# Reordering the down projection of a two-layer trunk: operand sums behind the seventh pair, an own buffer for a weight chunk, one low part on VectorE, and the first row's weighting

## The reference

```
h = RMSNorm(x);  z = h @ W_in
A = gMLP spatial gating;  B = differential attention
x = x + RMSNorm(concat(A, B) @ W_out)
h = RMSNorm(x);  gu = h @ W_gate_up         # 1024 -> 2 x 2816
y = (silu(gate) * up) @ W_down              # 2816 -> 1024
x = x + RMSNorm(y) * post_ffn_g
```

## Time and profile before

| | |
|---|---|
| median of 3 runs | 1087.85 us (1087.07 to 1088.01) |
| the profiled execution | 1088.94 us |
| its span, first to last instruction | 1087.1 us |
| mean granted TensorE clock, as a share of full speed | 0.995 |
| busy share: PE, DVE, ACT, POOL | 98%, 72%, 58%, 46% |
| down projection and its residual, layer 0 | about 423 to 545 us of the span |
| the same, layer 1 | 960 us to the end |

### The profile page before, as it was taken

The page is one execution under the profiler, slowest core; times in us unless marked ns, Lnnn a source line. Parts: engine busy times, 40 slices in busy tenths (PEclk is TensorE's granted clock), DMA queues, the critical chain, the costliest instruction groups (busy, mean ns, idle before and its releaser), DMA issues.

```text
span 1087.1 us, 17807 instructions
## 1 busy us (share of the span) xinstructions
PE 1064.4 (98%) x6704; PEld 950.4 (87%) x6704; DVE 781.7 (72%) x1267; ACT 632.3 (58%) x1253; POOL 501.8 (46%) x386
## 2 busy tenths in 40 slices
PE   9999999999999999999899999999999999999997
PEld 7888788999999999778678888889999999987775
DVE  4376554878888885978754756457888888869784
ACT  6767784755555554434457568656555555544361
POOL 3534364466666663020544344634766666610221
PEclk9999999999999999999999999999999999999999
DMA  9423113424433432664453222232343344336442
GB/s 297 139 61 108 65 59 88 145 79 117 117 109 88 115 118 78 225 210 160 141 159 104 78 78 78 78 129 85 99 118 107 90 115 116 95 121 233 154 165 77
DMA packets 151161, 130.39 MB, mean 120 GB/s; under 512 B 4250, under 2 KB 120484, under 8 KB 151076
## 3 DMA queue, kind: packets, MB, share of 16 engines
q1 hardware_dynamic: 151060, 129.25, 38.0%
q10 hardware_dynamic: 16, 0.00, 0.0%
HBM read 122.95 MB, written 6.29 MB: 119 GB/s over the span
## 4 chain that ended last, share of the span: by engine, by line
PE 81%; DVE 10%; DMA 3%; ACT 2%; POOL 2%; issue 2%; POOLq 0%; DVEq 0%; SPq 0%; ACTq 0%
PE banks L694 25%; PE banks L696 24%; PE banks L695 24%; DVE w_lo L2140 3%; DMA raw<-in_w_down_dram 2%; POOL w_lo L632 2%; PE banks L759 2%; PE banks L787 2%; PE banks L703 1%; PE banks L772 1%; PE banks L1012 1%; DVE raw L2127 1%; DVE raw L2129 1%; DVE part_full L2104 1%; DVE raw L2125 1%
## 5 line engine op out<-in xcount | busy, mean ns | idle before, releaser
L632 POOL TENSOR_TENSOR w_lo<-raw,w_hi 128x512 fp32r<-128x512 f32 x148 | 197.3, 1358 | 382.0 <-ACT w_hi L1222 382.0
L650 POOL TENSOR_TENSOR w_lo<-raw,w_hi 128x512 fp32r<-128x512 f32 x200 | 261.4, 1318 | 145.9 <-ACT w_hi L1303 141.5
L694 PE MATMUL banks<-xg_hi,w_hi 128*128 128x256 f32 (+1 forms) x880 | 273.5, 311 | 0.0
L696 PE MATMUL banks<-xg_lo,w_hi 128*128 128x256 f32 (+1 forms) x880 | 271.3, 308 | 0.0
L695 PE MATMUL banks<-xg_hi,w_lo 128*128 128x256 f32 (+1 forms) x880 | 271.2, 308 | 0.0
L1303 ACT ACTIVATE w_hi<-raw 128x512 fp32r<-128x512 f32 x200 | 124.6, 631 | 116.6 <-DVE raw L2034 64.2
L696 PEld LDWEIGHTS banks<-xg_lo,w_hi 128*128 128x128 f32 x880 | 168.1, 191 | 8.5
L694 PEld LDWEIGHTS banks<-xg_hi,w_hi 128*128 128x128 f32 x880 | 168.1, 191 | 8.2
L695 PEld LDWEIGHTS banks<-xg_hi,w_lo 128*128 128x128 f32 x880 | 168.1, 191 | 7.5
L696 PE MATMUL banks<-s_part,w_hi 128*128 128x256 f32 x480 | 135.8, 283 | 0.0
L694 PE MATMUL banks<-s_part,w_hi 128*128 128x256 f32 x480 | 135.8, 283 | 0.0
(11 more groups left out here) (225 smaller groups left out, 2175.0 us busy)
## 6 DMA issues: line engine op xcount, KB each, us to landing
raw<-in_w_gate_up_dram SPq DMA_DIRECT2D x88, 512.0 KB, 4.1
raw<-in_w_down_dram SPq DMA_DIRECT2D x58, 512.0 KB, 3.9
raw<-in_w_in_dram SPq DMA_DIRECT2D x40, 512.0 KB, 3.8
raw<-in_w_out_dram SPq DMA_DIRECT2D x16, 512.0 KB, 3.4
x_spill<-x_rows SPq DMA_DIRECT2D x8, 512.0 KB, 5.0
x_rows<-x_spill SPq DMA_DIRECT2D x8, 512.0 KB, 6.3
raw<-in_w_down_dram SPq DMA_DIRECT2D x14, 256.0 KB, 2.6
x_rows<-in_x_dram SPq DMA_DIRECT2D x4, 512.0 KB, 7.1
```

The lines of the kernel that those rows point to most:

```text
L632: last = tt(lo[:, piece], raw_half(l, c, h)[:, piece], hi[:, piece].bitcast(F32), ALU.subtract)
L650: tt(lo, full, hi.bitcast(F32), ALU.subtract).then_inc(w_ready, 1)
L694: mm(o, stat[0], mov[0], start=first, stop=False)
L696: return mm(o, stat[0], mov[1], start=False, stop=last)
```

## The change

- **Order on DVE.** `h_low(0)` moves behind the sums of P0. `h_low(1)`, `s4_sums(EARLY)` and `h_low(2)` move behind P6. `h_low(3)` moves behind the sums of Q0. On ACT `h_high(3)` moves behind L18's high parts and `keep_p1`.
- **R14's raw home.** Its halves no longer pass through `raw`: they have places of their own in `part_full`, are loaded right behind Q2 once P6's T3 product is done, and signal `r14_landed`. R18, now of kind Z, so follows Q6 in `raw` and reuses Q5's buffer. S1's high part moves one tile up and two buffers of `keep_p5` move, to make room.
- **Low part of R18's second half.** It is made on DVE (`late_low`, two pieces, semaphore `late_ready`), between `add_right(0)` and `add_p56(1)`. POOL then has six pieces for R14 and R18.
- **First row.** `gain_a` of row 2 runs behind the first row's add and that of row 3 behind its weighting, followed by `bias_a` for rows 2 and 3. `bias_a` for rows 0 and 1 comes with `gain_a` of those rows.

```diff
-        [("R", 14), ("R", 18)]
+        [("R", 14), ("Z", 18)]
...
+    C_R14 = C_DOWN + DOWN.index(("R", 14))
...
-                   "S1": (part_hi[:, NP:2 * NP, :], hid_hi[:, first_of_pair, right]),
+                   "S1": (part_hi[:, NP + 1:2 * NP + 1, :], hid_hi[:, first_of_pair, right]),
...
-        p5 = part_full[:, 0, 2 * NP:2 * NP + 2, :], part_full[:, 1, 2 * NP:2 * NP + 2, :]
+        p5 = part_full[:, 1, 2 * NP:2 * NP + 2, :], m1_full.rearrange("p (a q) -> p a q", a=2)
...
-        LOWS_OF = {"B": 5, "P": 0, "Q": 0, "W": 2, "L": 2, "R": 2}
+        LOWS_OF = {"B": 5, "P": 0, "Q": 0, "W": 2, "L": 2, "R": 2, "Z": 1}
...
+        RAW_ORDER = [(l, c) for l in range(L) for c in range(NC) if c != C_R14]
+
+        def raw_n(l, c):
+
+            return (NC - 1) * l + c - (c > C_R14)
+
         def raw_half(l, c, h):
-            return raw[:, (NC * l + c) % 2, h, :]
+            if c == C_R14:
+                return part_full[:, 0, 4 * h:4 * h + 4, :].rearrange("p n q -> p (n q)")
+            return raw[:, raw_n(l, c) % 2, h, :]
...
             def load_half(l, c, h):
-                n = NC * l + c
+                n = raw_n(l, c)
                 if n >= 2:
 
-                    m, d = divmod(n - 2, NC)
+                    m, d = RAW_ORDER[n - 2]
...
+                    elif d == LAST and h == 1:
+                        sp.wait_ge(late_ready, m + 1)
...
+            def load_r14(l):
+
+                sp.wait_ge(w_done, upto(l, C_P[NP - 1], P_T3))
+                for h in range(2):
+                    view, src = weights_of(l, C_R14, h)
+                    sp.dma_start(view(raw_half(l, C_R14, h)), src).then_inc(r14_landed[h], 16)
...
                 for c in range(C_DOWN + 2, NC):
+                    if c == C_R14:
+                        continue
                     load(l, c)
+                    if c == C_Q[2]:
+                        load_r14(l)
...
                     if not paired(c):
                         low(l, c, 0)
-                        low(l, c, 1)
+                        if c != LAST:
+                            low(l, c, 1)
...
-                pe.wait_ge(w_ready, low_upto(l, c, h))
+                if c == LAST and h == 1:
+                    pe.wait_ge(late_ready, l + 1)
+                else:
+                    pe.wait_ge(w_ready, low_upto(l, c, h))
...
-                    elif c == C_P[6]:
-                        h_high(3)
                     elif c == C_L_END:
                         keep_p1(0)
                         keep_p1(1)
+                        h_high(3)
...
-                if rows[-1] == ST - 1:
-                    ts(bias_a[:, :], ssq_a[:, :], 1.0 / D, EPS, ALU.mult, ALU.add).then_inc(bias_a_ready, 1)
+                if len(rows) > 1:
+                    add_eps(slice(rows[0], rows[-1] + 1))
+
+            def add_eps(at):
+
+                ts(bias_a[:, at], ssq_a[:, at], 1.0 / D, EPS, ALU.mult, ALU.add).then_inc(bias_a_ready, 1)
...
                     tt(y_b, y_b, silu_t[:, r, :], ALU.add).then_inc(y_b_added, 1)
+                    if r == 0:
+                        gain_a(b, (2,))
                 dve.wait_ge(ssq_b_ready, ST * b + r + 1)
                 tt(y_b, y_b, gpost[:, HALF:D], ALU.mult).then_inc(y_b_gained, 1)
+                if b % 2 and r == 0:
+                    gain_a(b, (3,))
+                    add_eps(slice(2, ST))
...
+                def late_low():
+
+                    hi, lo = high_low(l, LAST, 1)
+                    dve.wait_ge(w_hi_ready, upto(l, LAST, 1))
+                    for piece in (slice(0, CE // 2), slice(CE // 2, CE)):
+                        last = tt(lo[:, piece], raw_half(l, LAST, 1)[:, piece], hi[:, piece].bitcast(F32), ALU.subtract)
+                    last.then_inc(late_ready, 1)
...
-                h_low(0)
                 for p in range(NP):
                     pair_sums(C_P[p])
+                    if p == 0:
+                        h_low(0)
                     pair_lows(C_P[p])
                     if p < 2:
                         s2_sum(p)
-                    elif p == 4:
-                        h_low(1)
-                    elif p == 5:
-                        s4_sums(EARLY)
-                        h_low(2)
-                h_low(3)
+                s4_sums(EARLY)
+                h_low(1)
+                h_low(2)
                 add_p7(0)
                 add_p7(1)
                 pair_sums(C_Q[0])
+                h_low(3)
                 pair_lows(C_Q[0])
...
-                for j in range(2):
-                    add_p56(j)
-                    add_right(j)
+                add_p56(0)
+                add_right(0)
+                late_low()
+                add_p56(1)
+                add_right(1)
...
-                    gain_a(2 * l + 1, range(2, ST))
```

More of the change, by code:

```diff
@@ L128, in trunk @@
         silu_t = sb("silu_t", [P, 4, S])
-        m1 = sb("m1", [P, 512])[:, 0:256]
+        m1_full = sb("m1", [P, 512])
+        m1 = m1_full[:, 0:256]
         junk = sb("junk", [P, D], BF16)
@@ L335, in trunk @@
         p5_kept = sem("p5_kept")
+        late_ready = sem("late_ready")
+        r14_landed = [sem(f"r14_landed{h}") for h in range(2)]
         p56_added = sem("p56_added")
@@ L358, in paired @@
             return kind_of(c) in ("P", "Q")
-        DONE_OF = {"B": 7, "P": 4, "Q": 3, "W": 2, "L": 2, "R": 2}
-        LOWS_OF = {"B": 5, "P": 0, "Q": 0, "W": 2, "L": 2, "R": 2}
+        DONE_OF = {"B": 7, "P": 4, "Q": 3, "W": 2, "L": 2, "R": 2, "Z": 2}
+        LOWS_OF = {"B": 5, "P": 0, "Q": 0, "W": 2, "L": 2, "R": 2, "Z": 1}
         def count(l, c, i, each):
@@ L521, in weights_of @@
                 return lambda t: t[:, 0:SE], w_dn_v[l, :, 2 * n, 0:HALF]
-            half, k = (h, 2 * n) if kind in ("P", "Q") else (int(kind == "R"), n + 2 * h)
+            half, k = (h, 2 * n) if kind in ("P", "Q") else (int(kind != "L"), n + 2 * h)
             return wide, w_dn_v[l, :, k:k + 2, half * HALF:(half + 1) * HALF]
@@ L924, in down_part @@
                 elif k + 2 == FT:
-                    last.then_inc(y_b_done if kind == "R" else y_a_done, 1)
+                    last.then_inc(y_a_done if kind == "L" else y_b_done, 1)
             def pair_product(l, c, i, part, o, first, last):
@@ L1210, in high @@
             def high(l, c, h):
-                n = NC * l + c
-                act.wait_ge(raw_landed[n % 2][h], 16 * (n // 2 + 1))
+                n = raw_n(l, c)
+                if c == C_R14:
+                    act.wait_ge(r14_landed[h], 16 * (l + 1))
+                else:
+                    act.wait_ge(raw_landed[n % 2][h], 16 * (n // 2 + 1))
                 if home[l, c] is None:
@@ L1279, in root_of_branch @@
                 if r == 0:
-                    act.wait_ge(bias_a_ready, b + 1)
+                    act.wait_ge(bias_a_ready, 3 * (b // 2) + (2 if b % 2 else 1))
+                if r == 2 and b % 2:
+                    act.wait_ge(bias_a_ready, 3 * (b // 2 + 1))
                 act.wait_ge(ssq_b_ready, ST * b + r + 1)
@@ L1292, in factor_high @@
             def factor_high(l, f, i):
-                n = NC * l + C_GU + f
+                n = raw_n(l, C_GU + f)
                 if i in (B11, B21, B22):
@@ L1790, in boundary @@
                 group = b + 1
-                gain_a(b, range(2, ST) if b % 2 else range(ST))
+                if b % 2 == 0:
+                    gain_a(b)
                 for r in range(ST):
```

## The result

The changed kernel takes 1075.84 us (median, 1075.17 to 1076.15), the kernel before, measured beside it, 1087.78 (1087.07 to 1088.01). The ratio is 0.989 (95% interval 0.987 to 0.991): 11.9 us or 1.1% faster. The forecast was 1077.7 us. The profiled execution took 1076.15 us against 1088.94, a span of 1074.4 us against 1087.1.

A forecast was written before the change was run, and what follows sets the result against it. PE, busy 98%, was held to lose some 10.4 us a layer to down-projection stalls and half clock. Wins of 5.0 (layer 0) and 5.1 (layer 1) gave 1078.8 profiled, median 1077.7 us; forecast 1076.5 to 1079, 8-in-10 range 1069.7 to 1081.

The forecast's parts named there:

- part 1: P pairs: with DVE's new order all PE stalls there go, and L18 starts 5.8 us earlier in layer 1.
- The half clock: P pairs: behind the 2.3 us stall before P6, PE's clock halves for about 3.4 us, costing 1.6 us a layer.
- Part 2: L18 and Q pairs: turn-taking with POOL adds 5.0 us to DVE; PE waits 0.9, 0.9 (Q0's T2, Q2) and 0.25 (Q5).
- Part 3: First row: POOL starts R14 earlier, PE waits 2.4 us for R18's first half; 5.1 us are won in layer 1.
- Part 4: First row: the moved gains fit DVE's gaps at a cost of 0 to 0.2 us, avoiding a wait of up to 1.
- No lock at all: Rival, L18 and first row: DVE and POOL hardly disturb each other; 9.0 us a layer, 1069.8 us; chance 0.25 including its half.
- the lock at L18 alone: Half of that rival: DVE and POOL take turns only at L18; 6.5 us a layer, 1074.9 us; within the same 0.25.
- A clock that falls in the first row: Rival: the first row's 2.4 us stall halves the clock, 1.6 us for each layer; 1079.3 or 1080.9 us; chance 0.13.
- Late transfers: Rival, P pairs: P4's and P6's loads come late, part of the stalls returns, 1 to 2 us a layer; 1080 to 1082; chance 0.08.
- Slower through four falls of the clock: Rival, Q pairs and first row: four short stalls a layer each cost 1.6 us by half clock; 1090.4 us; chance 0.03.

The follow-up runs named there:

- part 1 undone: The changed kernel with DVE's old order and ACT's h_high(3) put back, the rest of the change kept: 1081.75 us, ratio 0.994 to the kernel before.
- part 1 alone: The kernel before with only the new order on DVE and ACT's h_high(3) moved: 1080.18 us, ratio 0.993.
- the best kernel: The changed kernel with h_low(1) behind P3's low parts, s4_sums(EARLY) behind P5's, and R14's second-half low part on DVE: 1068.90 us.

## Why the prediction was right, point by point

**The size.** 1075.84 us is inside the range of 8 in 10 (1069.7 to 1081) and outside the narrower forecast of 1076.5 to 1079. It is 1.9 us under the 1077.7 worked out; the terms that were booked too dear stand below.

**What bounds, and part 1: right.** PE reached L18 6.0 us earlier in layer 0 and 5.9 in layer 1 (worked out: 5.8); the low parts came in time for every P pair. DVE was through h_low(2) at 1008.0 us, which with the 5.8 us that this layer starts earlier is 1013.8 in the time of before; worked out was 1013.6.

**The half clock came and went with the execution, not with the stall.** I booked 1.6 us a layer as part of the stall's price. For the profiled execution of before the sum holds: both stretches are in its trace, and in each some eight matmuls start 0.43 us apart in the place of 0.227; none is in the trace after. As a reason it was wrong: the same stalls came back with part 1 undone, without it. Nor was it rare before. The mean granted clock of the 21 executions of before beside the experiments is 0.995 to 0.998, on average 0.9969. The 48 of the changed kernel and of the kernels without P stalls have 0.998 to 1.000, on average 0.9989. By an estimate from these, the 0.002 of 1087 us is about one stretch of 3.4 us at half clock in a typical execution of before, where the profiled one had two. That would also fit its standing 1.1 us above its median, while the one after stands 0.3 above its own. What drops the clock stays open.

**Part 2: right in mechanism, a little too dear.** The stalls at Q0's T2 and before Q2 were forecast as starts 0.9 us late each. In layer 1 the starts were 0.8 and 0.7 late (0.6 and 0.55 as idle time); in layer 0 the first was 0.25 late. The one at Q5 (0.25) didn't come; in its place layer 0 had one as small at Q6. In layer 1 the Q pairs then ended 0.5 us earlier than worked out. By taking POOL away, and by moving the steps away, the cause is shown: beside POOL each DVE instruction with two SBUF inputs took 1.0 to 1.1 us more here, and POOL's four pieces 4.1 together. The GPSIMD Engine Reference of the Trainium skill (section Key points) says that such instructions contend with GPSIMD; the trace agrees. That they take turns by whole instructions is read from the rows here.

**Part 3: the right stall, for the most part.** In layer 0 POOL started R14 at 510.95 us; 1047.4 less 536.5 is 510.9. R18's first half was used by PE at 519.43 against 519.9 worked out, after a wait of 1.7 us; one of 0.8 for R14's second half, put at 0.3, stood in front of it. In layer 1 the wait was 1.25, not 2.4: POOL started 0.8 us earlier than worked out, of which 0.3 because Q5's sums no longer waited for a load and 0.3 because DVE was through add_left that much earlier than worked out. And late_low's first piece came just behind POOL's fifth, so only one piece of DVE's stood before the sixth (2.96 us for POOL's two in the place of 3.9). This is where the forecast was off in size: 5.1 us worked out for layer 1, 7.0 measured; 5.0 for layer 0, 5.4 at the first row. The turns beside late_low were booked at 1.4 us for R18's first half and cost POOL's two pieces 0.9 in layer 0 and 0.45 in layer 1. Two more steps of the forecast went wrong in worth. The load of R14 was taken for the reason of POOL's earlier start; undoing it cost 0.9 us at most, as DVE's earlier chain alone moves that load too (with part 1 alone POOL starts R14 in layer 0 at 511.10 us, against 510.95 with all parts). And late_low was put down as 2.5 us off POOL: by POOL's rows it is worth 0.1 a layer, and the medians show no more (-0.1 and 0.4 us). The forecast's own numbers said so: eight pieces from 1047.4 on are done at 1057.45, before the 1057.9 at which it has R18's second half start.

**Part 4: right.** The gains fitted; the reciprocal came 0.3 us behind them, waiting for ACT. Changed kernel, layer 1: the gain of row 2, the weighting, the reciprocal.

```profile
1052.50 0.68 DVE L1788 TENSOR_TENSOR hid_full<-hid_full,gpost 128x512 f32<-128x512 f32 x1
1053.35 0.70 DVE L1810 TENSOR_TENSOR banks<-banks,gpost 128x512 f32<-128x512 f32 x1 [0.17 <-ACT junk L1309]
...
1055.02 0.17 DVE L1815 RECIPROCAL rs_y<-root_y 128x1 f32<-128x1 f32 x1 [0.30 <-ACT root_y L1316]
```

That the move only avoids a wait was right, and the wait shows once the first row comes early enough: 1.7 us in the best kernel.

**The rivals.** No lock at all: refuted. Its half, the lock at L18 alone, was forecast at 1074.9 us and came 0.9 from the measured time, nearer than the forecast (1.9), in part because the turns in the first row cost so much less than booked; but turns there were. A clock that falls in the first row: didn't happen. Late transfers: the loads left DVE idle 1.0 to 1.6 us, within the margins. Slower through four falls of the clock: none fell in the profiled execution.

## What to carry to other kernels

Work that is moved off a critical stretch lands beside something: look at what the other engines run there before counting it as free, and fill gaps in which an engine already waits for a load. Handing pieces from one engine to another that shares its access to SBUF is worth nothing while both want it at once, and pays in time in which the receiver idles. A part's worth is that in its neighbourhood: the own buffer and the moved gains were worth 0.9 us at most and 0 in this version and 3.4 and 1.7 in a faster one.

## What the runs showed of the hardware

A DVE instruction with two SBUF inputs beside back-to-back POOL pieces took 1.0 to 1.1 us more at three sizes (0.69 to 1.79 us for 128x512, 1.22 to 2.32 for 128x1024, 2.02 to 3.12 for 128x1792), which is nearly one POOL piece of 1.27 us, and each POOL piece waited for DVE's instruction in turn; DVE instructions with one input in a bank kept their 0.69. A PE stall of 2.26 us was followed by half clock for 3.4 us in one kernel's profile and one of 2.25 us at the same place by full clock in another's.
